# Feature-major input and output by the host, and the layer norms' root by Ln and Exp on ScalarE

## The reference

```python
def rms_norm(x, gain=None):
    xf = x.astype(jnp.float32)
    y = xf * lax.rsqrt(jnp.mean(xf * xf, axis=-1, keepdims=True) + NORM_EPS)
    ...
def reference(x_prompt, x_sample, ...):
    xp, xs = x_prompt, x_sample          # (1, 1024, 1024) and (8, 1, 1024)
    for i in range(DEPTH):
        hp = rms_norm(xp, norm_g[i])
        hs = rms_norm(xs, norm_g[i])
        ...                              # mixer i mod 3
        xp = xp + op.astype(xp.dtype)
        xs = xs + os_.astype(xs.dtype)
    return (xp, xs, ...)                 # and states, key and value rows
```

## Time and profile before

| | us |
|---|---|
| median of 3 runs | 3680.82 (3678.0 to 3686.5) |
| profiled execution | 3687.29 |
| its span, first to last instruction | 3685.5 |
| mean granted TensorE clock | 0.945 |
| busy: PE / PEld / DVE / ACT / POOL | 3283.7 / 2945.7 / 1456.4 / 1192.5 / 749.5 |

### The profile page before, as it was taken

How to read it: one execution, slowest core, us unless ns; L and a number is a source line. 1 busy time by engine, 2 the same in 40 slices (tenths; PEclk the granted TensorE clock), 3 DMA queues, 4 the chain that set the end, 5 groups by cost and what they waited for, 6 DMA issues and landing times.

```text
span 3685.5 us, 56759 instructions
## 1 busy us (share of the span) xinstructions
PE 3283.7 (89%) x20193; PEld 2945.7 (80%) x20193; DVE 1456.4 (40%) x3286; ACT 1192.5 (32%) x2294; POOL 749.5 (20%) x476
## 2 busy tenths in 40 slices
PE   4999999997996999999968799969799999999788
PEld 3979798886996777777747688859697979798688
DVE  4161514235234334344434566642515161514431
ACT  4232313223123444444432344531323232323211
POOL 3101111113333111110003322233311202011341
PEclk7999999997998999999987899979899999999799
DMA  3647465557212444444443012131124242424611
GB/s 110 226 141 253 141 229 164 198 183 236 90 43 71 128 130 131 130 133 136 136 134 119 18 57 73 56 105 39 39 87 142 86 139 86 129 91 129 226 60 68
DMA packets 512941, 450.90 MB, mean 122 GB/s; under 512 B 24598, under 2 KB 460598, under 8 KB 510674
## 3 DMA queue, kind: packets, MB, share of 16 engines
q1 hardware_dynamic: 406294, 325.75, 29.0%
q10 hardware_dynamic: 106428, 122.27, 9.9%
HBM read 348.56 MB, written 166.50 MB: 140 GB/s over the span
## 4 chain that ended last, share of the span: by engine, by line
PE 70%; DVE 11%; issue 6%; ACT 5%; POOL 4%; DMA 3%; SPq 1%; ACTq 0%; DVEq 0%; POOLq 0%
PE psum L266 17%; PE psum L267 17%; PE psum L268 17%; PE psum L861 3%; POOL Hl L291 3%; PE psum L857 3%; DVE hraw L367 2%; PE psum L1254 2%; ACT Hh L288 2%; PE psum L1227 2%; DMA arena<-scratch_kc 2%; PE psum L853 1%; DVE hraw L328 1%; PE psum L836 1%; PE psum L869 1%
## 5 line engine op out<-in xcount | busy, mean ns | idle before, releaser
L266 PE MATMUL psum<-Hh,Wh 128*128 128x384 f32 (+1 forms) x4896 | 1663.1, 340 | 185.4 <-POOL Hl L291 75.8
L267 PE MATMUL psum<-Hl,Wh 128*128 128x384 f32 (+1 forms) x4896 | 1602.4, 327 | 0.0
L268 PE MATMUL psum<-Hh,Wl 128*128 128x384 f32 (+1 forms) x4896 | 1601.4, 327 | 0.0
L266 PEld LDWEIGHTS psum<-Hh,Wh 128*128 128x128 f32 x4896 | 952.3, 195 | 242.6 <-issue 101.9
L242 POOL TENSOR_TENSOR Wl<-wraw,Wh 128x1024 fp32r<-128x1024 f32 (+1 forms) x208 | 495.2, 2381 | 2388.7 <-ACT Wh L238 2388.7
L267 PEld LDWEIGHTS psum<-Hl,Wh 128*128 128x128 f32 x4896 | 955.2, 195 | 13.9 <-issue 8.2
L268 PEld LDWEIGHTS psum<-Hh,Wl 128*128 128x128 f32 x4896 | 952.1, 194 | 0.0
L238 ACT ACTIVATE Wh<-wraw 128x1024 fp32r<-128x1024 f32 (+1 forms) x208 | 216.1, 1039 | 312.9 <-PE psum L268 224.1
L291 POOL TENSOR_TENSOR Hl<-hraw,Hh 128x384 fp32r<-128x384 f32 (+1 forms) x252 | 226.1, 919 | 327.5 <-ACT Hh L288 327.5
L376 DVE TENSOR_TENSOR xT<-psum,xT 128x384 f32<-128x384 f32 x168 | 86.3, 514 | 370.3 <-PE psum L268 369.8
L288 ACT ACTIVATE Hh<-hraw 128x384 fp32r<-128x384 f32 (+1 forms) x252 | 116.2, 488 | 261.2 <-DVE hraw L367 125.4
(11 more groups left out here) (216 smaller groups left out, 3183.0 us busy)
## 6 DMA issues: line engine op xcount, KB each, us to landing
wraw<-in_ret_w_in SPq DMA_DIRECT2D x96, 512.0 KB, 3.9
scratch_kc<-in_cache_kt SPq DMA_DIRECT2D x64, 512.0 KB, 6.3
scratch_vc<-in_cache_v SPq DMA_DIRECT2D x64, 512.0 KB, 7.0
arena<-in_state_ret ACTq DMA_DIRECT2D x64, 512.0 KB, 6.0
out_ret_state_sample<-arena ACTq DMA_DIRECT2D x64, 512.0 KB, 2.8
arena<-scratch_kc SPq DMA_DIRECT2D x64, 512.0 KB, 5.2
arena<-scratch_vc SPq DMA_DIRECT2D x64, 512.0 KB, 5.4
scratch_on<-arena ACTq DMA_DIRECT2D x80, 256.0 KB, 3.4
```

The costliest lines, as they stand in the source:

```text
L266: nc.tensor.matmul(out, hi, xh, start=(k == 0), stop=False)
L267: nc.tensor.matmul(out, hi, xl, start=False, stop=False)
L268: last = nc.tensor.matmul(out, lo, xh, start=False, stop=(k == kt - 1))
```

## The change

The host hands over x as `x_cols` (feature by token, prompt and sample together) and the gains as `norm_gp` (128 by 32), and turns the output `y_cols` back; keys and values are as before. On the chip:

- Six loads of four feature tiles by one chunk go straight into xT, with no wait between them. Transposes, copies, the additions into `ss` and the memset of `ss` are gone from the input.
- For layer 0, TensorE sums the squares: eight matmuls with `ones` per chunk, accumulated in NB, read `sqb0`, which now has a tile for each of the eight squares. The squares of chunk c+1 wait until the matmuls of chunk c have read them.
- In all twelve chunk norms ScalarE computes Ln and then Exp with scale -0.5; VectorE's reciprocal is gone. Ahead of a layer's first chunk a load of the table set that holds both functions is placed.
- SP stores xT by feature tile, a tile as soon as its last residual addition is done; the last tile goes out by chunk.

```diff
         def norm_act(act, layer, c):
...
-            act.activation(rst[:, 0:w], NB[:, 0:w], ACT.Sqrt, bias=eps_t[:, 0:1], scale=1.0 / D_MODEL)\
-               .then_inc(nrm_sq, 1)
+            if c == 0:
+                act.preload_act_table_set("natural_log_exp_and_others")
+            act.activation(rst[:, 0:w], NB[:, 0:w], ACT.Ln, bias=eps_t[:, 0:1], scale=1.0 / D_MODEL).then_inc(nrm_ln, 1)
+            act.wait_ge(nrm_ln, n + 1)
+            act.activation(rst[:, 0:w], rst[:, 0:w], ACT.Exp, scale=-0.5).then_inc(nrm_sq, 1)
             fill_parts(act, None, None, f, c)
...
             dve.wait_ge(nrm_sq, norm_index(layer, c) + 1)
-            ch.link(nc.vector.reciprocal(rst[:, 0:w], rst[:, 0:w]))
...
         def input_sp(sp):
             sp.sem_inc(raw_free, CR)
...
             sp.dma_start(ptab[0:1, :], A["page_table"].rearrange("(a b) p -> a (b p)", a=1)).then_inc(tab_ld, 16)
...
+            for c in range(NC_):
+                c0, w = CHUNKS[c]
+                for half in range(2):
+                    k0 = 4 * half
+                    src = A["x_cols"][k0 * P:(k0 + 4) * P, c0:c0 + w].rearrange("(k p) t -> p k t", p=P)
+                    sp.dma_start(xT[:, k0:k0 + 4, c0:c0 + w], src).then_inc(xin_ld[2 * c + half], 16)
+                if c == 0:
                     load_w(sp, Pos(0), 0, w_block(A["ret_w_in"][0], 0, KT, RQK))
+                    sp.dma_start(ng[:, :, :].rearrange("p l k -> p (l k)"), A["norm_gp"]).then_inc(const_ld, 16)
+                    sp.dma_start(ident[:, :], A["c_ident"]).then_inc(const_ld, 16)
...
         def input_pe(pe):
+            for c in range(NC_):
+                c0, w = CHUNKS[c]
+                if c:
+                    pe.wait_ge(nrm_sq, c)
+                for k in range(KT):
+                    pe.wait_ge(sq_done, KT * c + k + 1)
+                    last = nc.tensor.matmul(NB[:, 0:w], ones[:, :], sqb0[:, k, 0:w], start=(k == 0), stop=(k == KT - 1))
+                last.then_inc(nrm_ps, 1)
             pe.wait_ge(const_ld, 32)
...
         def input_act(act):
             for c in range(NC_):
                 c0, w = CHUNKS[c]
...
+                if c:
+                    act.wait_ge(nrm_ps, c)
                 for k in range(KT):
...
+                    if k % 4 == 0:
+                        act.wait_ge(xin_ld[2 * c + k // 4], 16)
+                    act.activation(sqb0[:, k, 0:w], xT[:, k, c0:c0 + w], ACT.Square).then_inc(sq_done, 1)
                 if c:
                     norm_act(act, 0, c - 1)
...
+            def sp_(sp):
                 for k in range(KT):
...
+                    for c0, w, c in [(0, T, NC_ - 1)] if k < KT - 1 else [(*CHUNKS[c], c) for c in range(NC_)]:
+                        sp.wait_ge(unit_ev, ev_val(q_end - KT + k, c))
+                        sp.dma_start(A["y_cols"][k * P:(k + 1) * P, c0:c0 + w], xT[:, k, c0:c0 + w]).then_inc(y_st, 16)
+                sp.wait_ge(y_st, 16 * (KT - 1 + NC_))
+            return sp_
```

More of the change, by code:

```diff
@@ L302, in norm_pe @@
             n = norm_index(layer, c)
-            pe.wait_ge(ss_done, KT * NC_ * layer + (KT - 1) * NC_ + c + 1 if layer else KT * (c + 1))
-            if n:
-                pe.wait_ge(nrm_sq, n)
+            pe.wait_ge(ss_done, KT * NC_ * layer + (KT - 1) * NC_ + c + 1)
+            pe.wait_ge(nrm_sq, n)
             nc.tensor.matmul(NB[:, 0:w], ones[:, :], ss[:, c0:c0 + w], start=True, stop=True).then_inc(nrm_ps, 1)
@@ L390, in trunk @@
         al = arena()
[L391 to L398, removed]
+        sqb0 = al.take(KT, WMAX)
+        xin_ld = sems("xin_ld", 2 * NC_)
         def input_sp(sp):
             sp.sem_inc(raw_free, CR)
-            sp.dma_start(ident[:, :], A["c_ident"]).then_inc(const_ld, 16)
-            sp.dma_start(ngr[0:32, :], A["norm_g"].rearrange("l (k p) -> (l k) p", p=P)).then_inc(const_ld, 16)
@@ L411, in input_sp @@
                     load_w(sp, Pos(0), 0, w_block(A["ret_w_in"][0], 0, KT, RQK))
-        def input_blocks(c):
-            return [(0, 1, 2), (3, 4, 5), (6, 7, 8)][c]
+                    sp.dma_start(ng[:, :, :].rearrange("p l k -> p (l k)"), A["norm_gp"]).then_inc(const_ld, 16)
+                    sp.dma_start(ident[:, :], A["c_ident"]).then_inc(const_ld, 16)
         def input_pe(pe):
-            pe.wait_ge(const_ld, 32)
[L419 to L434, removed]
@@ L436, in input_evac @@
-        def input_evac(b, half):
-            w = P if b < NBLK else NS
-            src = xin_bank(b, half)[:, :].rearrange("p (k t) -> p k t", k=4)[:, :, 0:w]
-            return xT[:, 4 * half:4 * half + 4, b * P:b * P + w], src
+            for c in range(NC_):
[6 more added lines that the diff above has]
+                last.then_inc(nrm_ps, 1)
@@ new lines, in input_dve, with output_parts @@
+                for half in range(2):
+                    dve.wait_ge(xin_ld[2 * c + half], 16)
+                norm_dve(dve, ch, 0, c)
+        def output_parts(layers):
+            y_st = sem("y_st")
+            q_end = UNIT_AT[layers - 1] + [RET_UNITS, DIFF_IN + DIFF_OUT, LRU_IN + LRU_OUT, RET_UNITS][layers - 1]
+            def sp_(sp):
+                for k in range(KT):
+                    for c0, w, c in [(0, T, NC_ - 1)] if k < KT - 1 else [(*CHUNKS[c], c) for c in range(NC_)]:
[3 more added lines that the diff above has]
+            return sp_
@@ L2013 @@
     arrays, A = {}, {}
-    laid = {name: value for name, value in inputs.items() if name != "cache_k"}
+    laid = {name: value for name, value in inputs.items() if name not in ("cache_k", "x_prompt", "x_sample", "norm_g")}
+    xs = _np.concatenate([_np.asarray(inputs["x_prompt"])[0], _np.asarray(inputs["x_sample"])[:, 0]], axis=0)
+    laid["x_cols"] = _np.transpose(xs)
+    laid["norm_gp"] = _np.transpose(_np.asarray(inputs["norm_g"]).reshape(4, KT, P), (2, 0, 1)).reshape(P, 4 * KT)
     laid["cache_kt"] = _np.transpose(_np.asarray(inputs["cache_k"]), (0, 1, 3, 4, 2))
@@ L2029 @@
     out["v_rows_sample"] = v_tok.reshape(1, NS, 1, DH, DV)
+    y_tok = _np.ascontiguousarray(_np.transpose(_np.asarray(out["y_cols"]).reshape(D_MODEL, T)))
+    out["y_prompt"] = y_tok[0:SEQ].reshape(1, SEQ, D_MODEL)
+    out["y_sample"] = y_tok[SEQ:T].reshape(NS, 1, D_MODEL)
     return tuple(out[name] for name in ("y_prompt", "y_sample", "ret_state_prompt", "ret_state_sample", "k_rows_prompt",
```

88 lines of the change are left out of this document (7 added, 81 removed).

## The result

The changed kernel takes 3622.9 us (median of 4 runs, 3622.5 to 3625.7), the kernel before 3682.1 in the same comparison (4 runs, 3678.0 to 3686.5): ratio 0.9841, 95% interval 0.9824 to 0.9858. The profiled execution took 3622.67 us, its span is 3620.9 (before: 3687.29 and 3685.5), so the two traces differ by 64.6 us.

A forecast was written before the change was run, and what follows sets the result against it. TensorE was taken as busy inside the layers, idle at start, three norms and end; 13.4 + 16.2 + 15.4 = 45.0 us off the median 3680.8 gave 3635.8, likeliest 3636, range 3627 to 3648.

The forecast's parts named there:

- Norms: Norms ahead of layers 1, 2 and 3: Ln and Exp without the reciprocal save 5.3, 4.7 and 3.4 us, 13.4 together.
- the 0.55 us lost to GpSimd in the third chunk: Later norms, chunk 2: VectorE's multiplications meet GpSimd's subtractions, so 0.85 of 1.4 us stay; bounds of the effect 0 and 0.9.
- the table load of layer 3: Norm ahead of layer 3: a new load of 1.28 us, nothing beyond it; chunk 0 gains 0.7 instead of 2.0 us.
- Start: From the input to layer 0's first unit: that unit's chain moves 16.2 us sooner, bounds 12 to 18.
- the first sums: Start, chunk 0's sums of squares on TensorE: first matmul at 13.65, 8.0 us long, ready at 21.65.
- The chunks started: Start, VectorE's three chunks: begin 10.2, 15.4 and 16.2 us sooner, the last after 0.5 lost to GpSimd's subtraction.
- End: After the last residual addition: only the last tile's third chunk is left to store, 15.4 us saved, bounds 14.5 and 16.
- Inside the layers TensorE works without a break: Layers 0 to 3: idle time touched lies only at start, norms and end, so the layers add nothing to the sum.
- x was not late: Rival at the start: x loads follow at 3.9 us per 512 KB, start gains 5 not 16.2 us, 3647 us; 6%.
- The weight loads landed: Rival in layer 0: weight loads behind page copies take over their 16 us, slower if landings reach 17.2 us; 2%.
- TensorE keeps the high clock at the norms: Rival: in shorter pauses TensorE keeps its clock, worth half of 5.3 us at one or two places, 3631 us; 8%.
- a longer stretch behind 67 us: Sign of error: the forecast would be wrong if the stretch between 67 us and the first later norm grew.

The follow-up runs named there:

- experiment 1: Changed kernel with 69 increments of an unused semaphore ahead of TensorE's first wait: 3637.75 us, ratio 0.9871 to the kernel before.
- (2): Kernel before with 187 semaphore increments ahead of TensorE's first wait: 3693.23 us, ratio 1.0025 to the kernel before.
- the input alone: Kernel before with only the input changed (x and gains laid out by the host, sums of squares on TensorE): 3664.65 us, ratio 0.9943.
- items 1 to 5: Runs on the changed kernel or the kernel before: increments added, root, input or output changed alone, page copies moved; 3629.5 to 3693.23 us.
- 4: Changed kernel with 79 and with 49 semaphore increments ahead of TensorE's first wait, one run each: 3646.6 and 3629.5 us.
- 5: Kernel before with each head's first page copies a unit later: 3684.75 us, ratio 0.9998; changed kernel with 144 semaphore increments: 3651.96 us, one run.

## Why the prediction was wrong

- **Norms**, 13.4 forecast, 14.1 measured. Each norm came within 0.4, the 0.55 us lost to GpSimd in the third chunk (measured 0.44) and the table load of layer 3 included. Nothing beyond the load was paid: Ln starts 0.01 us behind it at 2567.82. The Trainium skill, "ScalarE: Activation LUTs", section "What ACT_TABLE_LOAD costs", has 2.66 us per switch with the drain; by it this norm would have gained 2.0 and not 3.5; the trace doesn't agree.
- **Start**, 16.2 forecast, 17.6 measured. Two errors in the first sums cancelled by luck: they began at 14.17 and not 13.65 and took 7.52 us instead of 8.0, so they ended at 21.69, as forecast (21.65). The chunks started 10.4, 16.0 and 17.2 us sooner (10.2, 15.4 and 16.2 forecast); what came on top came with the second and third chunk. A term slightly small.
- **End**, 15.4 forecast, 14.9 measured. Right.
- **The step that failed** is the first paragraph's "Inside the layers TensorE works without a break", and with it that nothing else would move when the ends are cut: the layers stood in the sum with nothing. TensorE had six breaks by issue at the jumps of layers 0 and 3 that I could have read in the kernel before, and in layer 0 three of them were followed by another after nine matmuls. What sets these second ones is where a loop lies in TensorE's code, and removing 69 instructions at the start moved that. The stalls themselves are 7.8 us, with the stretch behind them 10.1 by the traces. From the medians the size comes out as 11 to 15 (experiment 1, by how the start and the two comparisons are reckoned), 7.8 (2) and 18.6 - 10.4 = 8.2 us (the input alone), each uncertain by several us. (TensorE's other breaks in the layers, such as the waits for a ring at an output projection, one of 4.12 us in layers 0 and 3 that is listed as issue, are nearly the same before and after.)
- **The rest of the miss**, some 5 us in layer 0 and about 3 in layers 1 to 3 of the traces, goes at least in part with TensorE's clock behind the 2.96 us wait at the heads' ends. It was low in five of eight heads before, in one after, in one to five in the experiments of items 1 to 5. No experiment ties this to the change, and kernels without a second stall have it in one head or in four; by the medians, which differ by 59.2 and not by 64.6, part of it is the profiled execution's own (3687.29 against a median of 3682.14). Why it falls in one head and not in the next stays open.
- Rivals: x was not late (the first sums ended when forecast). The weight loads landed after 4.2 us in the median and 10.5 at most, before 4.0 and 11.7, far from the 16 that they have. That TensorE keeps the high clock at the norms didn't show: the second norm's mean was 0.75, before 0.72. The prediction's own sign of error, a longer stretch behind 67 us, was looked for on one side only: the stretch shrank.

The Trainium skill, page "Runtime: NRT & Kernel Launch", section "Instruction fetch mechanics", has a rule that would have warned: code comes in blocks of 16 KB, 256 instructions, TensorE's memory for it has room for 2048, and a taken branch whose target isn't in the current window of two pages has to wait for a fetch. The traces agree on the packets of 16 KB and on the wait at the jumps of the head loops, some 2380 instructions long by my count. They don't agree with a window of two pages: layer 1's and 2's loops are some 1440 and 650 instructions long, and in the kernel before no packet of code moves from 1293 to 1861 us, where layer 1's jumps back five times, and no break by issue over 0.2 us follows a jump of the two loops. This fits the 2048. That a loop which starts near its block's end waits a second time, the page doesn't say; experiments 1, 4 and 5 show it.

## What to carry over

When code is taken out ahead of a loop that is fetched again at each jump (here one of 2380 instructions), the loop's place against the 16 KB pieces moves, and its cost per jump changed by 1.6 to 3.4 us here, with no dependence between the two. Look in the kernel before for breaks by "issue" at loop jumps, count the matmuls behind them, and see whether packets of the queue named instruction move there. And a forecast for the ends of a kernel needs one pass over the middle: every wait there that no term of the sum names is a place where the difference can change.

## What was not expected of the hardware

- After a jump to code that has to be brought in, the first piece costs 1.5 to 2.1 us of standing still, and a second stall ended 3.5 to 5.2 us behind the first matmul, with the DMA engines at a share of 0.53 or of 1.07. The packets themselves took 0.9 to 1.5 us.
- One increment of a semaphore takes 0.15 us in TensorE's queue (the mean step between them in both traces): 187 of them held it until 29.52 us, 144 until 22.94.
- A VectorE instruction of 0.75 us took 2.82 each of the eight times that it met GpSimd's split of 2.34 us; it cost TensorE 2.96 us per head, 24 in all, and was gone by moving eight small matmuls.
